# Transposing attention probabilities on VectorE and by on-chip DMA instead of on TensorE

## The reference

```python
mod = jax.nn.silu(c) @ w_ada + b_ada
shift, scale, gate = jnp.split(mod, 3, axis=-1)
h = rmsnorm(x, g_norm) * (1.0 + scale[:, None, :]) + shift[:, None, :]
proj = h @ w_in                                   # 1024 -> 4096
q, k, v, z_attn, b_g, c_g, h_c, z_conv = jnp.split(proj, splits, axis=-1)
q = rope(q.reshape(B, S, N_HEADS, HEAD_DIM), positions).transpose(0, 2, 1, 3)   # 8 heads of 64
k = rope(k.reshape(B, S, N_HEADS, HEAD_DIM), positions).transpose(0, 2, 1, 3)
y_attn = moba_attention(q, k, v).transpose(0, 2, 1, 3).reshape(B, S, D_ATTN)
y_attn = rmsnorm(y_attn, g_attn_out) * jax.nn.silu(z_attn)
y_conv = short_gated_conv(b_g, c_g, h_c, w_conv)  # b_g * conv of width 3 over (c_g * h_c)
y_conv = rmsnorm(y_conv, g_conv_out) * jax.nn.silu(z_conv)
y = jnp.concatenate([y_attn, y_conv], axis=-1) @ w_out
out = rmsnorm(x + gate[:, None, :] * y, g_final)
```

## Time and profile before

| | us |
|---|---|
| median of 3 runs | 269.43 (268.59 to 269.57) |
| the profiled execution's own time | 269.49 |
| its span in the profile | 267.7 |
| TensorE busy | 257.7 |
| VectorE busy | 210.9 |
| ScalarE busy | 137.2 |
| GpSimd busy | 116.6 |

### The profile page before, as it was taken

One profiled execution on the slowest core, in us unless ns is written; L12 is line 12 of the kernel. 1 busy time (PEld: TensorE's weight loads), 2 busy tenths in 40 slices (PEclk: granted clock), 3 DMA queues, 4 the chain that ended last, 5 costly groups with the idle time before them and its releaser, 6 DMA issues.

```text
span 267.7 us, 3634 instructions
## 1 busy us (share of the span) xinstructions
PE 257.7 (96%) x1252; PEld 211.7 (79%) x1252; DVE 210.9 (79%) x337; ACT 137.2 (51%) x230; POOL 116.6 (44%) x71
## 2 busy tenths in 40 slices
PE   4999999999999999999999999999999999999991
PEld 1578888888788888888888888888888888888881
DVE  5799999799999976969969675924495569999554
ACT  5875576646097533591644723556927751310543
POOL 3410000558333433093366332337667975590440
PEclk9999999999999999999999999999999999999998
DMA  6999996698604642049463112532842592000034
GB/s 204 400 418 428 413 423 234 233 339 230 220 2 157 154 160 82 0 151 369 115 174 121 51 45 78 157 82 78 250 143 81 205 413 86 3 0 0 23 138 157
DMA packets 13220, 46.96 MB, mean 175 GB/s; under 512 B 2065, under 2 KB 2705, under 8 KB 11922
## 3 DMA queue, kind: packets, MB, share of 16 engines
q1 hardware_dynamic: 12912, 46.46, 49.8%
q10 hardware_dynamic: 290, 0.27, 0.3%
HBM read 40.43 MB, written 2.10 MB: 159 GB/s over the span
## 4 chain that ended last, share of the span: by engine, by line
PE 91%; DMA 2%; ACT 1%; POOL 1%; issue 1%; SPq 1%; DVE 0%; POOLq 0%
PE ps L1105 22%; PE ps L1107 22%; PE ps L1106 22%; PE ps L1190 5%; PE ps L1267 3%; PE ps L1255 3%; PE ps L1213 2%; PE ps L1205 2%; DMA xt<-in_x 2%; PE ps L1211 2%; PE ps L1203 2%; PE ps L1281 2%; PE ps L1274 2%; ACT x_junk L339 1%; POOL w_hi L639 1%
## 5 line engine op out<-in xcount | busy, mean ns | idle before, releaser
L645 POOL TENSOR_TENSOR w_lo<-raw,w_hi 128x1024 fp32r<-128x1024 f32 x29 | 75.0, 2596 | 104.5 <-ACT w_hi L361 69.2
L1105 PE MATMUL ps<-h_lo,w_hi 128*128 128x512 f32 x200 | 79.0, 395 | 0.0
L1107 PE MATMUL ps<-h_hi,w_hi 128*128 128x512 f32 x200 | 78.0, 390 | 0.0
L1106 PE MATMUL ps<-h_hi,w_lo 128*128 128x512 f32 x200 | 77.9, 390 | 0.0
L1107 PEld LDWEIGHTS ps<-h_hi,w_hi 128*128 128x128 f32 x200 | 37.5, 188 | 8.0
L1105 PEld LDWEIGHTS ps<-h_lo,w_hi 128*128 128x128 f32 x200 | 37.5, 188 | 7.9
L1106 PEld LDWEIGHTS ps<-h_hi,w_lo 128*128 128x128 f32 x200 | 37.6, 188 | 7.4
L361 ACT ACTIVATE w_hi<-raw 128x1024 fp32r<-128x1024 f32 x29 | 30.4, 1051 | 3.1 <-DMA raw<-in_wslots 3.1
L451 ACT ACTIVATE probs<-probs,rmin 128x384 f32<-128x384 f32 (+3 forms) x32 | 17.6, 550 | 14.0 <-DVE rmin L898 14.0
L908 DVE TENSOR_SCALAR probs<-probs,prec 128x384 f32<-128x384 f32 (+3 forms) x32 | 20.7, 709 | 0.3
L898 DVE CUSTOM_DVE_ANT_0 probs<-mask,ps 128x384 f32<-128x384 f32 (+3 forms) x32 | 13.4, 483 | 4.3 <-PE ps L1255 4.3
(11 more groups left out here) (158 smaller groups left out, 486.2 us busy)
## 6 DMA issues: line engine op xcount, KB each, us to landing
raw<-in_wslots SPq DMA_DIRECT2D x33, 512.0 KB, 3.4
ada<-in_ada SPq DMA_DIRECT2D x10, 1024.0 KB, 11.8
raw<-in_whead SPq DMA_DIRECT2D x7, 448.0 KB, 9.8
xt<-in_x SPq DMA_DIRECT2D x4, 512.0 KB, 5.8
ada<-in_ada SPq DMA_DIRECT2D x4, 512.0 KB, 8.3
qd<-qt SPq DMA_DIRECT2D x16, 128.0 KB, 2.3
kd<-kt SPq DMA_DIRECT2D x16, 128.0 KB, 2.3
x<-in_x SPq DMA_DIRECT2D x4, 512.0 KB, 5.8
```

Source lines behind the costliest of these rows:

```text
L645: nc.gpsimd.tensor_tensor(lo, src[:, :], hi.bitcast(F32), ALU.subtract).then_inc(s_lo, 1)
L1105: nc.tensor.matmul(o, a_hi, b_lo, start=start, stop=False)
L1106: nc.tensor.matmul(o, a_lo, b_hi, start=False, stop=False)
L1107: return nc.tensor.matmul(o, a_hi, b_hi, start=False, stop=stop)
```

## The change

The ten transposes of each head on TensorE go. In their place VectorE transposes the whole 128x1280 tile of probabilities in place, in blocks of 32x32 (`nc.vector.transpose`, behind `normalise`). SP then moves it to another buffer with four DMAs, each from 32 partitions to all 128 (`move_probs`), so that each block of keys gets into its place. To make blocks of 32 end up right, the keys are kept in another order: `key_order` lets ScalarE and VectorE read K with a step of four, and the mask and the rows of probabilities (`token_row`) are laid out in four runs per partition. `values` has five products with each part, whose operand and result are read and written in runs of 32 columns.

The probabilities' buffers are laid out again. Raw transposed probabilities of head 0 have a buffer of their own, in which the low part is later written in place; head 1's are written over head 0's original ones, and its high part over its own original ones. `probs_high` and `probs_low` read SBUF instead of PSUM. `probs_high` waits for the landing of the move and for the values of the pair before. `MOVES` puts the moves into SP's order, behind the load of the slot that it names.

```diff
@@ the tables
-    T_AT = {0: 0, 1: 512, 3: 896, 2: 1024}
+    SLOT = {0: 2, 1: 0, 2: 3, 3: 6}
+    QUAD, RUN = 32, 320
+    MOVES = {8: [(0, 0)], 10: [(0, 1)], 13: [(1, 0)], 16: [(1, 1)], 20: [(2, 0), (2, 1)], 26: [(3, 0), (3, 1)]}
+    VALUES = [(0, 0, 2, 2), (0, 1, 2, 2), (1, 1, 1, 3), (2, 2, 1, 2), (3, 3, 1, 1)]
@@ buffers
-        probs = [sb(f"probs{h}", [TRI]) for h in range(2)]
-        pt_hi, pt_lo = sb("pt_hi", [TRI], F32R), sb("pt_lo", [TRI], F32R)
+        place = [room(4 * TRI) for _ in range(4)]
+        probs = [at(f"probs{h}", place[h], [TRI]) for h in range(2)]
+        pt_raw = [at(f"pt_raw{h}", place[2 - 2 * h], [TRI]) for h in range(2)]
+        pt_lo = [at(f"pt_lo{h}", place[2 - 2 * h], [TRI], F32R) for h in range(2)]
+        pt_hi = [at(f"pt_hi{h}", place[3 - 2 * h], [TRI], F32R) for h in range(2)]
@@ new functions
+        def key_order(k):
+            return k[:, :].rearrange("p (j c b) -> p b j c", b=4, c=QUAD)
+        def token_row(i, h):
+            return probs[h].rearrange("p (b f) -> p b f", b=4)[:, :, SLOT[i] * QUAD:(SLOT[i] + i + 1) * QUAD]
+        def key_tile(pt, j, first, step, count):
+            a, each = SLOT[first] + j, SLOT[first + step * (count - 1)] - SLOT[first]
+            each = each // (count - 1) if count > 1 else 1
+            return pt.rearrange("p (b s c) -> p b s c", b=4, c=QUAD)[:, :, a:a + each * (count - 1) + 1:each, :]
+        def query_tiles(o, first, step, count):
+            return o.rearrange("p (i a c) -> p a i c", a=4, c=QUAD)[:, :, first:first + step * (count - 1) + 1:step, :]
@@ SP
+            def move_probs(p, h):
+                sp.wait_ge(p_quad, 2 * p + h + 1)
+                sp.wait_ge(pv_out, 2 * p)
+                if h:
+                    sp.wait_ge(p_moved[0], 64 * p + 64)
+                for a in range(4):
+                    sp.dma_start(pt_raw[h][:, a * RUN:(a + 1) * RUN], probs[h][a * QUAD:(a + 1) * QUAD, :]
+                                 ).then_inc(p_moved[h], 16)
             for n in range(NSLOT):
                 load_raw(KT + n, wslots_d[n], D)
+                if n in MOVES:
+                    for p, h in MOVES[n]:
+                        move_probs(p, h)
@@ ScalarE, probs_high
-                act.wait_ge(p_tr, 2 * p + h + 1)
-                act.wait_ge(pv_out, 2 * p + h)
-                nc.scalar.activation(pt_hi[:, :], ps[:, TB:TB + TRI], ACT.Copy).then_inc(p_hi, 1)
+                act.wait_ge(p_moved[h], 64 * p + 64)
+                act.wait_ge(pv_out, 2 * p)
+                nc.scalar.activation(pt_hi[h][:, :], pt_raw[h][:, :], ACT.Copy).then_inc(p_hi, 1)
@@ VectorE, least, normalise and probs_low
-                    dve.wait_ge(p_tr, 2 * (p - 1) + h + 1)
+                    dve.wait_ge(pv_out, 2 * p)
...
                 ins.then_inc(p_norm, 1)
+                dve.wait_ge(p_norm, 2 * p + h + 1)
+                nc.vector.transpose(probs[h][:, :], probs[h][:, :]).then_inc(p_quad, 1)
...
-                nc.vector.tensor_tensor(pt_lo[:, :], ps[:, TB:TB + TRI], pt_hi[:, :].bitcast(F32), ALU.subtract
+                nc.vector.tensor_tensor(pt_lo[h][:, :], pt_raw[h][:, :], pt_hi[h][:, :].bitcast(F32), ALU.subtract
@@ TensorE, score
-                    pe.wait_ge(p_lo, 2 * p)
@@ TensorE, transpose_probs (with its eight calls) and values
-            def transpose_probs(p, h):
-                pe.wait_ge(p_norm, 2 * p + h + 1)
-                if h == 0:
-                    pe.wait_ge(row_min, 8 * p + 8)
-                for i in range(TT):
-                    for j in range(i + 1):
...
-                        ins = nc.tensor.transpose(ps[:, o:o + P], probs[h][:, a:a + P], ident[:, :])
-                ins.then_inc(p_tr, 1)
...
-                for j in range(TT):
-                    nc.tensor.matmul(bank(2 + h, j * P, BANK), v2[:, j, 2 * p + h, :],
-                                     pt_hi[:, T_AT[j]:T_AT[j] + S - j * P], start=(j == 0), stop=False)
+                for n, (j, *tiles) in enumerate(VALUES):
+                    nc.tensor.matmul(query_tiles(y, *tiles), v2[:, j, 2 * p + h, :], key_tile(pt_hi[h][:, :], j, *tiles),
+                                     start=(n == 0), stop=False)
```

More of the change, by code:

```diff
@@ L195, in build @@
         scores, row_min, exps, rec_ok, p_norm = sem("scores"), sem("row_min"), sem("exps"), sem("rec_ok"), sem("p_norm")
-        p_tr, p_hi, p_lo, pv_out = sem("p_tr"), sem("p_hi"), sem("p_lo"), sem("pv_out")
+        p_quad, p_hi, p_lo, pv_out = sem("p_quad"), sem("p_hi"), sem("p_lo"), sem("pv_out")
+        p_moved = [sem(f"p_moved{h}") for h in range(2)]
         y_tmp, y_attn, za_ok, ya_gated = sem("y_tmp"), sem("y_attn"), sem("za_ok"), sem("ya_gated")
@@ L622, in _ @@
             pool.wait_ge(pool_step, 3)
-            nc.gpsimd.affine_select(out=mask[:, S - P:S], in_=mask[:, S - P:S], compare_op=ALU.is_ge, fill=MASKED,
-                                    base=0, pattern=[[-1, P]], channel_multiplier=1).then_inc(mask_ok, 1)
+            last = mask[:, :].rearrange("p (b f) -> p b f", b=4)[:, :, P - QUAD:]
+            nc.gpsimd.affine_select(out=last, in_=last, compare_op=ALU.is_ge, fill=MASKED,
+                                    base=0, pattern=[[-1, 4], [-4, QUAD]], channel_multiplier=1).then_inc(mask_ok, 1)
             for m in range(TT):
@@ L850, in k_low @@
                 dve.wait_ge(dup_k, 64 * p)
-                nc.vector.tensor_tensor(kt[:, 1], rk[:, :], kt[:, 0].bitcast(F32), ALU.subtract).then_inc(qk_lo, 1)
+                to, hi = (kt[:, i].rearrange("p (b j c) -> p b j c", b=4, c=QUAD) for i in (1, 0))
+                nc.vector.tensor_tensor(to, key_order(rk), hi.bitcast(F32), ALU.subtract).then_inc(qk_lo, 1)
             def value_low(m):
@@ L897, in least @@
                     e = 4 * h + n
[L898 to L899 removed]
+                    behind = mask[:, :].rearrange("p (b f) -> p b f", b=4)[:, :, P - w // 4:]
+                    score = ps[:, SB[h] + a:SB[h] + a + w].rearrange("p (b f) -> p b f", b=4)
+                    dve.tensor_tensor_reduce(token_row(i, h), behind, score, 1.0, 3.0e38, ALU.add, ALU.min,
+                                             rmin[:, e:e + 1]).then_inc(row_min, 1)
             def normalise(p, h):
@@ L1272, in values @@
                 pe.wait_ge(row_min, 8 * p + 8)
-                for j in range(TT):
-                    nc.tensor.matmul(bank(2 + h, j * P, BANK), v2[:, j, 2 * p + h, :],
-                                     pt_hi[:, T_AT[j]:T_AT[j] + S - j * P], start=(j == 0), stop=False)
+                y = bank(2 + h)
+                for n, (j, *tiles) in enumerate(VALUES):
+                    nc.tensor.matmul(query_tiles(y, *tiles), v2[:, j, 2 * p + h, :], key_tile(pt_hi[h][:, :], j, *tiles),
+                                     start=(n == 0), stop=False)
                 pe.wait_ge(p_lo, 2 * p + h + 1)
-                for j in (3, 0, 1, 2):
-                    m = HD if j in (3, 0) else P
-                    ins = nc.tensor.matmul(bank(2 + h, j * P, BANK, p0=0, p1=m), v2[:, j, 2 * p + h, 0:m],
-                                           pt_lo[:, T_AT[j]:T_AT[j] + S - j * P], start=False, stop=(j == 2))
+                for n, (j, *tiles) in enumerate(VALUES[-1:] + VALUES[:-1]):
+                    m = HD if n < 2 else P
+                    ins = nc.tensor.matmul(query_tiles(bank(2 + h, p0=0, p1=m), *tiles), v2[:, j, 2 * p + h, 0:m],
+                                           key_tile(pt_lo[h][:, :], j, *tiles), start=False, stop=(j == 2))
                 ins.then_inc(pv_out, 1)
```

27 lines of the change are left out of this document (8 added, 19 removed).

## The result

The changed kernel takes 278.28 us (median of 4 runs, 274.67 to 279.62) against 269.38 before: a ratio of 1.027 [1.020, 1.034]. The forecast was 266.9, and 270.5 the upper end of its range, so both sign and range were wrong. The profiled execution took 277.78 us with a span of 275.7, 8.0 more than before. What follows is read from this one execution; another of the same kernel took 274.67 us, with a span of 272.7 and a mean granted clock of 0.985 in place of 0.972. An estimate from these two spans and clocks is that it had some 7 us less at the lower clock.

The account below looks back on a forecast made before the run. The prediction took TensorE, 91% of the chain, as the bound. Its terms, -8.7 + 0.3 + 0.45 + 2.1 + 0.1 + 3.1 = -2.65 us from 269.5, gave 266.9 us, range 262.5 to 270.5.

Parts of the forecast that it names:

- The rest moves as one: Behind the attention: projections have their weights some 4 us early, so everything after shifts by the summed -2.65 us.
- The K copies ... I take nothing: K copies reading every fourth word: up to 0.7 us more each, taken as nothing because VectorE is not awaited there.
- ZA0: Unit in pair 0 writing the bank that rope K1 empties; rope waits behind a new VectorE transpose: stall 0.45 us.
- The low half of (0,1) ... hidden by 0.6: Pair 0, head 1: VectorE's low half ends at 95.7 and is wanted at 96.3, so no stall.
- Rival 2: No change: GpSimd wins races at (0,1), stall 1.7, and (1,1), 1.4; 270.0 us, or about 268.5; 17 in 100.
- Pair 1, 2.1: Low half of (1,0): VectorE, delayed by the transpose of (1,1), is done at 129.15; TensorE arrives at 127.05; stall 2.1 us.
- Pair 3, 3.1: Halves of (3,1), behind GpSimd's slot 25, load 28 and ScalarE's slots 27 and 28: TensorE stalls 3.1 us.
- Pair 2, 0.1: Low half of (2,0), late for want of its high half: TensorE arrives just as it ends, stall 0.1 us.
- rival 3: Slower: VectorE's block transposes run at half rate, 2.9 us each, giving 273.3 us; 12 in 100.
- the saving of 8.7: TensorE's chain: eight times ten transposes removed, 1.09 us for each ten, 8.7 us in all.
- rival 4: Slower: runs of 32 columns double the time of the values' products, giving 276.2 us; 6 in 100.
- the 0.3 for one more instruction each: Values' products on TensorE, five for four: up to 0.02 us per added instruction, 16 products, 0.3 us.

Follow-up runs that it names:

- e6_idle2: Kernel before the change, with TensorE waiting ahead of unit C3 for two small DMAs in series: 275.12 us, ratio 1.022.
- e9_load27: Changed kernel with the move of (3,1) behind load 27 in SP's queue instead of ahead of it: 276.5 us, ratio 1.024.
- e1_fill: Changed kernel with unused filler products on TensorE ahead of its four long waits: 276.59 us, ratio 1.025.
- e13_sums: Changed kernel with its operations reordered, the low half of (2,1) on GpSimd and one low part of the convolution's output on VectorE: 267.77 us, ratio 0.993.
- e3_knat: Changed kernel with K read in natural order instead of every fourth word, so its result differs: 275.81 us, ratio 1.023.
- e7_pool: Changed kernel with the low halves of (0,1), (1,0), (1,1) and (2,1) on GpSimd instead of VectorE: 278.65 us, ratio 1.033.
- e8_all: e7_pool with five more steps reordered on VectorE, SP and ScalarE: 274.1 us, ratio 1.017.

## Why the prediction was wrong

**The step that failed: "The rest moves as one", with each stall priced at its length.** No term stands for TensorE's clock behind a stall. Forecast and profiled span are 10.65 us apart (-2.65 against +8.0), and by the balance 5.4 of them are clock; e6_idle2 shows the term by itself. The prediction's own stalls of 2.1 and 3.1 us were long enough to ask. With falls of 3.41 to 6.83 us behind these two, 1.6 to 3.2 us each, the forecast would have been between no change and 4 us slower.

**The other half, 4.5 us more waits and 1.0 for the breaks:**
- *"The K copies ... I take nothing"*: 0.4 and 0.5 us each, on the way to ZA0 (0.45 forecast, 1.02 measured, 0.45 without the stride) and to (0,1), where what they cost isn't shown. The Trainium skill (SBUF — State Buffer, "Specifications (TRN2)") says that lines are 16 bytes and that two hits in one are needed for full rate; a stride of four fp32 words has one. This case's rows agree, with 1052 against 684 ns, and the prediction had the upper bound (0.7) but not this reason for it.
- *"The low half of (0,1) ... hidden by 0.6"*: measured 2.16 of wait. Rival 2 has the mechanism, with 1.7; it was given 17 in 100 with all that it needs. The same program won the race in e9_load27 (0.54), so that it was lost in the profiled execution is in part luck, and a forecast would have had to give both ends a fair chance.
- *Pair 1, 2.1*: measured 2.50, the mechanism right. But TensorE was 4.35 us and VectorE 4.7 us later than forecast (131.40 for 127.05, 133.84 for 129.15), behind pair 0's waits and its fall, so that the two agree owes something to luck.
- *Pair 3, 3.1*: measured 3.80 + 0.56, the mechanism right, and load 28's 4.9 us in place of 3.4 the most of the difference. *Pair 2, 0.1*: 0.24.

**Right:** the transposes (1.5 forecast, 1.51 measured, rival 3 out), no contention of theirs with GpSimd, the saving of 8.7, the products (rival 4 out; the 0.3 for one more instruction each doesn't show). On these products the Trainium skill (PSUM — Partial Sum Buffer, "Specifications (TRN2)") has any non-contiguous pattern slow; runs of 32 fp32 words didn't, 0.59 us against 0.57 to 0.59. Four issues of a move were 2.60 and not 2.41.

**Left open:** how a loss divides between the clock's price and the waits. The balance gives the clock 5.4 us, but e1_fill, which took every fall away, was 276.59 us, not 5.4 faster. What remains if the waits are gone as well is shown by e13_sums alone. There, of the 8.7 us spared, 4.2 go to waits and about 1.3 to their eight breaks, which leaves 3.2; the spans differ by 2.1, and the missing 1.1 wasn't followed up.

## What to carry to other kernels

Where an engine is the chain at 91% and its neighbours fill their gaps to within a microsecond, shortening it makes an order wrong that was right: ask for each wait what stands ahead of the instruction waited for, and put the one that is asked for first in front. Price a stall of TensorE by its length and, where it may reach 2 us, by a fall of the clock as well (the counts are below). Where a VectorE instruction and a GpSimd one start within half a microsecond of each other, take both ends of the race into the forecast. Here fillers kept the clock and not the time. And take the profile of more than one execution before a wait is called the change's own.

## What the runs showed of the hardware

- **The clock behind a wait.** Over all runs and behind the first 15 us, TensorE has nine waits of 3.2 to 5.0 us, and all nine had a stretch at 1.2 GHz in or behind them; ten of 2.0 to 2.6 us, and five had (2.13, 2.16, 2.19, 2.31, 2.50) where five had none (2.06, 2.12, 2.25, 2.32, 2.58); none under 2.0 had one. (A fall in the last 4.1 us of every execution, the kernel before included, isn't counted.) A stretch took 3.41 or 6.83 us, and these runs show no rule for which.
- **VectorE and GpSimd.** At (0,1) one of the two is stretched: VectorE's 1.48 us to 3.10 (after) and 3.06 (e1_fill), or GpSimd's 2.4 to 5.45 (e3_knat), 5.40 (e9_load27) and 4.94 (e13_sums). In all five GpSimd's instruction began ahead of the low half, by 0.01 to 1.00 us, so this alone doesn't decide. What goes with the outcome is whether it also began ahead of VectorE's sum just before (L961): by 0.03 and 0.40 us in the first two, while it began 0.09 to 0.59 us behind it in the other three. With five cases this is a sign and no proof.
- **Four scalings under GpSimd** took 6.70 us before and after, to the digit. Under GpSimd's third instruction (e7_pool, e8_all) they took 9.4. The block transposes, with one operand, kept to 1.51 us.
